# Stick attention masked and summed in one PSUM bank, the delta rule's halves in buffers and a chain of their own, and new words

## The reference

```
z = einsum('bhqd,bhkd->bhqk', qb, k) * scale          # 8 heads of 64
strict = k_pos[None, :] < q_pos[:, None]
log_beta = log_sigmoid(z)
log_keep = where(strict, log_sigmoid(-z), 0.0)
later = cumsum(log_keep, axis=3, reverse=True) - log_keep
w = where(strict, exp(log_beta + later), 0.0)
out = einsum('bhqk,bhkd->bhqd', w, v)
```

## Time and profile before

| | |
|---|---|
| median of 3 runs | 2432.87 us (2431.02 to 2443.61) |
| the profiled execution | 2449.8 us, of which the span from first to last instruction is 2448.0 us |
| TensorE, matmul busy | 2325.2 us (95%), 14918 records |
| VectorE, ScalarE, GpSimd busy | 1556.2 us (64%), 1135.5 us (46%), 430.6 us (18%) |
| chain that ended last | TensorE 87%, VectorE 7%, ScalarE 4%, issue 2% |
| mean granted TensorE clock | 0.966 of full speed |
| mean busy share of the 16 DMA engines | queue 1, 35% of their span |

### The profile page before, as it was taken

How to read it: one execution, slowest core, us unless ns; L and a number is a source line. 1 busy time by engine, 2 the same in 40 slices (tenths; PEclk the granted TensorE clock), 3 DMA queues, 4 the chain that set the end, 5 groups by cost and what they waited for, 6 DMA issues and landing times.

```text
span 2448.0 us, 37895 instructions
## 1 busy us (share of the span) xinstructions
PE 2325.2 (95%) x14918; PEld 2059.4 (84%) x14918; DVE 1556.2 (64%) x2791; ACT 1135.5 (46%) x2015; POOL 430.6 (18%) x393
## 2 busy tenths in 40 slices
PE   6999999899999999999999889999998998999997
PEld 6888879888888889998888777888888886888886
DVE  6866756587687668557765763546765664345765
ACT  5654563365465453436544422336544522244553
POOL 2420012122122100022200320001221030000223
PEclk9999999999999999999999998989998999799998
DMA  6554413154554541125554103014543301102552
GB/s 245 187 177 148 160 36 121 67 191 179 185 190 181 183 158 68 53 87 196 184 185 149 61 19 114 1 69 160 189 173 114 133 27 72 44 23 97 183 181 86
DMA packets 88738, 310.53 MB, mean 127 GB/s; under 512 B 9840, under 2 KB 12144, under 8 KB 88048
## 3 DMA queue, kind: packets, MB, share of 16 engines
q1 hardware_dynamic: 88272, 305.42, 35.1%
q10 hardware_dynamic: 288, 2.69, 0.3%
HBM read 307.02 MB, written 1.05 MB: 126 GB/s over the span
## 4 chain that ended last, share of the span: by engine, by line
PE 87%; DVE 7%; ACT 4%; issue 2%; POOL 1%; DMA 0%; SPq 0%; DVEq 0%; ACTq 0%; POOLq 0%
PE ps L142 85%; DVE scratch L157 3%; PE ps L147 2%; DVE w_lo L157 1%; ACT w_hi L152 1%; ACT scratch L152 1%; DVE scratch L184 1%; ACT L152 1%; ACT scratch L183 1%; DVE scratch L169 1%; POOL scratch L157 0%; ACT h L152 0%; DVE scratch L163 0%; ACT x L152 0%; DMA ring<-in_w 0%
## 5 line engine op out<-in xcount | busy, mean ns | idle before, releaser
L157 DVE TENSOR_TENSOR w_lo<-ring,w_hi 128x1024 fp32r<-128x1024 f32 (+2 forms) x571 | 693.9, 1230 | 431.1 <-ACT w_hi L152 420.7
L142 PE MATMUL ps<-h,w_hi 128*128 128x512 f32 (+1 forms) x2784 | 876.9, 374 | 31.1 <-DVE h L169 19.0
L152 ACT ACTIVATE w_hi<-ring 128x1024 fp32r<-128x1024 f32 (+2 forms) x571 | 582.5, 1033 | 510.0 <-PE ps L142 502.3
L142 PE MATMUL ps<-h,w_lo 128*128 128x256 f32 x2448 | 690.7, 282 | 0.0
L142 PEld LDWEIGHTS ps<-h,w_hi 128*128 128x128 f32 x2784 | 506.7, 191 | 131.5 <-issue 23.5
L142 PEld LDWEIGHTS ps<-h,w_lo 128*128 128x128 f32 x2448 | 466.9, 191 | 0.0
L142 PE MATMUL ps<-f,w_hi 128*128 128x512 f32 (+1 forms) x1444 | 421.9, 358 | 3.3 <-DVE f L157 3.3
L142 PE MATMUL ps<-f,w_lo 128*128 128x256 f32 x1184 | 333.2, 281 | 0.0
L142 PE MATMUL ps<-consts 128*128 128x128 f32 x2374 | 319.1, 286 | 0.0
L142 PEld LDWEIGHTS ps<-consts 128*128 128x128 f32 x2374 | 299.8, 200 | 14.9 <-issue 9.9
L142 PE MATMUL ps<-scratch 64*128 64x128 f32 (+11 forms) x2016 | 284.8, 314 | 24.4 <-DVE scratch L157 10.1
(11 more groups left out here) (130 smaller groups left out, 2273.5 us busy)
## 6 DMA issues: line engine op xcount, KB each, us to landing
ring<-in_w SPq DMA_DIRECT2D x520, 512.0 KB, 3.3
ring<-in_w SPq DMA_DIRECT2D x48, 384.0 KB, 3.4
ring<-in_w SPq DMA_DIRECT2D x16, 396.0 KB, 5.0
stage_consts<-in_ctwo ACTq DMA_DIRECT2D x1, 1344.0 KB, 5.9
stage_consts<-in_cthree ACTq DMA_DIRECT2D x1, 1281.0 KB, 5.5
stage_consts<-in_cone SPq DMA_DIRECT2D x1, 1211.0 KB, 6.0
ring<-in_w SPq DMA_DIRECT2D x9, 128.0 KB, 2.7
x<-in_x SPq DMA_DIRECT2D x4, 256.0 KB, 4.3
```

What stands on the lines that cost most here:

```text
L142: return self.e.matmul(out, lhsT, rhs, start=start, stop=stop, skip_group_check=free)
L152: return self.e.activation(out, x, func, **k)
L157: return self.e.tensor_tensor(out, a, b, op)
```

## The change

- **Stick attention.** `qb` is scaled by 1/8 when it is evicted. z stays in its bank through step 1: TensorE adds the mask (`strict` is now 0 or -1e30, copied to fp32r on ScalarE once) by a product with the identity; ScalarE makes a = Ln(1 + Exp(-Abs(z))); VectorE makes a = max(z, 0) + a in one instruction; TensorE adds its sums over later keys, with the key itself, negated (`lower`, `ones`), onto z in the same bank; ScalarE takes Exp of it. The second bank, the clamp, VectorE's difference and sum and GpSimd's two masks are gone.
- **Delta rule.** A `DeltaBlock` for each half holds its masked products, inverse and what follows from it; some buffers are shared within it (N2, A4, Zt lie on N8; A2, Td on A8), so the copy of the first product of `ri` 0 waits for the second product too. `rm`, `ri`, `ru` of half 1 are a chain of their own, s. Pt, Q moved to the start of scratch; GpSimd clears them at `ri` 0 in place of `rm` 0, and waits for the block's column products first.
- **Words.** All six are new, with 1021 z: m0 80, c0 85, m1 189, c1 77, b0 281, b1 309. In m0, `ck` 1 to 4 come ahead of the stick attention's first head.

```
-SW = 31000
+SW = 31768
-NCON = 3584
+NCON = 2688
 WEAVE = {
...
-    "m0": ("zzzzpzzzzqzyqzzzzzzzzzzqzkzzzzzkzzzqzpzzzzzkqzzbzzzbzkzzalbvtvkasbbaacbzzzaszctaazcctzsszzatyczz"
-           "zzzstccaatszszzztyzzczzszzzazzzcczzzztazsszzzzzzzztzczczzzzozzzzzzzyyzzzyzzzzzzzzzzzzzzztzzzzzs"
-           "zzzzzzzzzzzzzzzzzzyzyooztsoozoozzzzzooozooooozzzozzzozzzozzzzz"),
...
+    "m0": ("zzpzzzyzzqqzkzzqzzzzzkzzpzzbqbkyqzzzzzzzzzzzzzzzyzzlzbykyakvayvbcaasbtcbycsztacaastcsacytszcatsc"
+           "azccattascztctzzzzzzozzzstszzzzzzzzszzzzootstosozzzozozozoooozzzozzzoozoozozzzz"),
...
-        self.strict = K.const("strict", lambda I: np.concatenate(
-            [np.triu(np.ones((128, 128)), 1), np.ones((128, 128)), np.triu(np.ones((128, 128)), 1)], 1), 384, "one")
-        self.lower = K.const("lower", lambda I: np.tril(np.ones((128, 128)), -1), 128, "one")
-        self.ones = K.const("ones", lambda I: np.ones((128, 128)), 128, "one")
+        self.strict = K.const("strict", lambda I: np.where(np.triu(np.ones((128, 128)), 1), 0.0, NEG), 128, "one")
+        self.lower = K.const("lower", lambda I: -np.tril(np.ones((128, 128))), 128, "one")
+        self.ones = K.const("ones", lambda I: -np.ones((128, 128)), 128, "one")
...
         q, k = T.sq(h), T.sk(h)
-        e.mm(b[:, 0:256], k[:, 0:128], q, True, True)
-        e.mm(b[:, 256:384], k[:, 128:256], q[:, 128:256], True, True).then_inc(*e.up("scores", ("stick", h)))
+        e.wait_ge(*K.at("masks", "strict"))
+        e.mm(b[:, 0:256], k[:, 0:128], q, True, False, free=True)
+        e.mm(b[:, 256:384], k[:, 128:256], q[:, 128:256], False, False, free=True)
+        e.mm(b[:, 0:384].rearrange("p (a k) -> p a k", a=3)[:, 0:3:2, :], K.ident_r, bc(K.strict_r, 2), False, False,
+             free=True).then_inc(*e.up("scores", ("stick", h)))
     elif step == 1:
-        b = K.bank(e, ATT, ("stick", h, "c"))
+        b = K.psum(("stick", h, "z"))
         e.wait_ge(*K.at("kept", ("stick", h)))
-        e.mm(b[:, 0:256], T.lower, a[:, 0:256], True, False, free=True)
-        e.mm(b[:, 128:256], T.ones, a[:, 256:384], False, True, free=True)
-        e.mm(b[:, 256:384], T.lower, a[:, 256:384], True, True, free=True).then_inc(*e.up("summed", ("stick", h)))
+        e.mm(b[:, 0:256], T.lower, a[:, 0:256], False, False, free=True)
+        e.mm(b[:, 128:256], T.ones, a[:, 256:384], False, False, free=True)
+        e.mm(b[:, 256:384], T.lower, a[:, 256:384], False, True, free=True).then_inc(*e.up("summed", ("stick", h)))
...
 def act_stick(e, K, T, h, step):
     a, l = (x[:, 0:384] for x in T.sticks[h % 2])
+    z = K.psum(("stick", h, "z"))[:, 0:384]
     if step == 0:
-        e.wait_ge(*K.at("clamped", ("stick", h)))
+        e.wait_ge(*K.at("scores", ("stick", h)))
         if h >= 2:
             e.wait_ge(*K.at("summed", ("stick", h - 2)))
-        e.then(e.act(a, K.psum(("stick", h, "z"))[:, 0:384], ACT.Abs, scale=64 ** -0.5))
+        e.then(e.act(a, z, ACT.Abs))
         e.then(e.act(a, a, ACT.Exp, scale=-1.0))
         e.act(a, a, ACT.Ln, bias=K.onec).then_inc(*e.up("logs", ("stick", h)))
     elif step == 1:
-        e.wait_ge(*K.at("evicted", ("stick", h, "c")))
-        e.act(l, l, ACT.Exp).then_inc(*e.up("exps", ("stick", h)))
+        e.wait_ge(*K.at("summed", ("stick", h)))
+        if h >= 2:
+            e.wait_ge(*K.at("weighted", ("stick", h - 2)))
+        e.act(l, z, ACT.Exp).then_inc(*e.up("evicted", ("stick", h, "z")))
...
 def dve_stick(e, K, T, h, step):
-    a, l = (x[:, 0:384] for x in T.sticks[h % 2])
-    sc = 64 ** -0.5
+    a = T.sticks[h % 2][0][:, 0:384]
     if step == 0:
-        z = K.psum(("stick", h, "z"))[:, 0:384]
-        e.wait_ge(*K.at("scores", ("stick", h)))
-        if h >= 2:
-            e.wait_ge(*K.at("weighted", ("stick", h - 2)))
-        e.ts(l, z, sc, 0.0, MUL, MIN).then_inc(*e.up("clamped", ("stick", h)))
         e.wait_ge(*K.at("logs", ("stick", h)))
-        e.then(e.tt(l, l, a, SUB))
-        e.stt(a, z, -sc, l, MUL, ADD).then_inc(*e.up("evicted", ("stick", h, "z")))
-    elif step == 1:
-        e.wait_ge(*K.at("summed", ("stick", h)))
-        e.tt(l, l, K.psum(("stick", h, "c"))[:, 0:384], ADD).then_inc(*e.up("evicted", ("stick", h, "c")))
-    else:
+        e.stt(a, K.psum(("stick", h, "z"))[:, 0:384], 0.0, a, MAX, ADD).then_inc(*e.up("kept", ("stick", h)))
+    elif step == 2:
...
+class DeltaBlock:
+    def __init__(self, K, at, G):
+        m3 = lambda i: K.area(at + 512 * i, 512, j=4, t=128)
+        self.M = {n: m3(i) for i, n in enumerate(("N8", "A8", "Ao16", "Ao32", "Rb", "Rk", "Ak"))}
+        self.P1 = m3(7)
+        self.N2 = self.A4 = self.Zt = self.M["N8"]
+        self.A2 = self.Td = self.M["A8"]
...
+        self.by_block = [DeltaBlock(K, OVER + 4608 * i, K.rows[:, 256 * i:256 * i + 256]) for i in range(2)]
...
+        inner = lambda tb: ([("rm", (tb, n)) for n in range(5)] + [("ri", (tb, n)) for n in range(7)]
+                            + [("ru", (tb, n)) for n in range(2)])
+        r += inner(0)
         for tb in range(2):
-            r += ([("rm", (tb, n)) for n in range(5)] + [("ri", (tb, n)) for n in range(7)] + [("ru", (tb, n)) for n in range(2)]
-                  + [("rG", tb)] + [("rP", (tb, j)) for j in range(2)] + [("rS", (tb, c)) for c in range(4)]
+            r += ([("rG", tb)] + [("rP", (tb, j)) for j in range(2)] + [("rS", (tb, c)) for c in range(4)]
                   + [("rY", (tb, j)) for j in range(2)])
-        return {"r": r + some("rO", 2),
+        return {"r": r + some("rO", 2), "s": inner(1),
...
-            e.wait_ge(*K.at("summed", key(m)))
+            e.wait_ge(*K.at("summed", key(2 if m == 1 else m)))
...
-            e.wait_ge(*(K.at("summed", (s, "rY", 0, 1)) if tb else K.at("turned", (s, "rtm", 3))))
+            e.wait_ge(*K.at("turned", (s, "rtm", 3)))
...
-    elif what == "rm" and i == (0, 0):
+    elif what == "ri" and i == (0, 0):
         e.wait_ge(*K.at("turned", (s, "rtm", 3)))
+        for n in [(s, "rp", 4), (s, "gp", 2), (s, "gl")] + [((s, "np", n), t) for n in range(3) for t in range(2)]:
+            e.wait_ge(*K.at("summed", n))
```

More of the change, by code:

```diff
@@ L242, in __init__ @@
         self.vf = make("v_first", 512)
-        mr = make("mask_r", 256, F32R)
-        self.ident_r, self.mask_r = mr[:, 0:128], mr[:, 128:256]
+        mr = make("mask_r", 384, F32R)
+        self.ident_r, self.mask_r, self.strict_r = (mr[:, 128 * i:128 * i + 128] for i in range(3))
         self.st = make("stats", 384)
@@ L1549, in pe_stick @@
         v = lambda k: T.vb[:, k, 64 * h:64 * h + 64]
-        e.wait_ge(*K.at("weights", ("stick", h)))
+        e.wait_ge(*K.at("evicted", ("stick", h, "z")))
         for t in range(2):
@@ L1563, in act_mixer0 @@
             act_masks(e, K, "chunk", T.chunk)
+            e.cp(K.strict_r, T.strict).then_inc(*e.up("masks", "strict"))
     elif what in ("lqa", "lka", "lva", "lvb") and i == 1:
@@ L1614, in dve_mixer0 @@
         e.wait_ge(*K.at("evicted", (T.stage, "R")))
-        evict_cols(e, K, (T.stage, what, i), (T.qbT if what == "qb" else T.kbT)[:, 2 * i:2 * i + 2, :], R=K.R)
+        if what == "qb":
+            e.wait_ge(*K.at("summed", (T.stage, what, i)))
+            b = K.psum((T.stage, what, i))[:, :].rearrange("p (k t) -> p k t", k=2)
+            e.stt(T.qbT[:, 2 * i:2 * i + 2, :], b, 64 ** -0.5, bc(K.R, 2), MUL,
+                  MUL).then_inc(*e.up("evicted", (T.stage, what, i)))
+        else:
+            evict_cols(e, K, (T.stage, what, i), T.kbT[:, 2 * i:2 * i + 2, :], R=K.R)
     elif what in ("qa", "ka"):
@@ L1684, in pool_mixer0 @@
         pool_x(e, K, T.stage, i)
-    elif what == "S":
-        h, step = i
-        a, l = (x[:, 0:384] for x in T.sticks[h % 2])
-        if step == 0:
-            e.wait_ge(*K.at("evicted", ("stick", h, "z")))
-            e.tt(a, a, T.strict, MUL).then_inc(*e.up("kept", ("stick", h)))
-        elif step == 1:
-            e.wait_ge(*K.at("exps", ("stick", h)))
-            e.tt(l, l, T.strict, MUL).then_inc(*e.up("weights", ("stick", h)))
 class Mla:
@@ L1899 @@
 OVER = 9744
-GN = 19472
+GN = 20240
 def block_mask(n, kind):
@@ L2057, in __init__, with block_of @@
                        lambda u: [])
+    def block_of(self, what, i):
+        return self.by_block[i if what == "rG" else i[0] if what in ("rm", "ri", "ru", "rP", "rS", "rY") else 0]
     def chains(self):
@@ L2238, in pe_delta @@
 def pe_delta(e, K, T, what, i, xT):
-    s, l, M = T.stage, T.l, T.M
+    s, l, V = T.stage, T.l, T.block_of(what, i)
+    M = V.M
     if what == "rp":
@@ L2312, in pe_delta @@
             e.wait_ge(*K.at("evicted", key(4)))
-            each(e, b, T.A4, T.P1).then_inc(*e.up("summed", key(5)))
+            each(e, b, V.A4, V.P1).then_inc(*e.up("summed", key(5)))
         elif n in (3, 5):
@@ L2326, in pe_delta @@
             e.wait_ge(*K.at("evicted", key((n - 1, "tr"))))
-            each(e, b, T.Td, T.Zt).then_inc(*e.up("summed", key((n, "r7"))))
```

(7 more changed lines are left out.)

99 lines of the change are left out of this document (46 added, 53 removed).

## The result

The changed kernel takes 2414.83 us (median of 5; 2408.71 to 2417.53) against 2431.24 for the kernel before on the same chip: a ratio of 0.9915, interval 0.9893 to 0.9937, so 16 us less by the medians and 21 by the ratio. A second set of runs gives 0.9929 (0.9911 to 0.9948), 17 us less. The forecast was 2387 and its range ended at 2413. The sign was right, the size was not: the time lies in the range of rival B.

The account below looks back on a forecast made before the run. TensorE, with fill on its path, was taken as the bound; m0 -4, c0 -1, m1 -8, c1 -3, b0 -17, b1 -15, clock +2 gave -46: 2387 us against the median 2432.87. Forecast 2376 to 2402, whole range 2362 to 2413.

Parts of the forecast that it names:

- rival B: Engines behind TensorE (VectorE in the blocks, ScalarE in m0, m1) take back half or more: 2403 to 2421 us, chance 0.18.
- what the fill's time is worth: All stages: 249 fewer fill products issued, at 0.225 us each, give 56 us at most.
- These stay: b0 and b1: the short stretches at 1.2 GHz, as behind `nc`'s products, stay; 2 us added for m0's new waits only.
- The count of fill: Issued z fall by 79 (m0), 6 (c0), 42 (m1), 15 (c1), 53 (b0), 54 (b1): 249 in all.
- m0, forecast -4: m0, stick attention: 79 fill products fewer, 1.8 us of mask products and 12 us of new waits added: -4 us.
- ScalarE late next: m0's packed heads: ScalarE has 36 us of work against TensorE's 33; followed head by head, 12 us of new waits.
- b0, forecast -17: b0, delta rule halves: 12 us from less fill and 5 us from bare waits gained: -17 us.
- The gap between 1417 and 1467: b0: second-half pieces fill TensorE's waits there; of 10 us of bare waits 5 are gained, VectorE late next.
- b1, forecast -15: b1, delta rule halves: 10.5 us from less fill and 4.5 us from bare waits gained: -15 us.
- b1 over 365 us: Sign that the prediction is wrong: b0 or b1 takes over 365 us.
- m1, c0, c1, forecast -12: m1, c0, c1: order and fill alone, nothing computed differently: -8, -1 and -3 us.
- D's mechanism: From `nc` to the output product of b0, b1: less fill puts more small products at 1.2 GHz; slower, chance 0.05.

Follow-up runs that it names:

- e_trim_m1: e_ck_between with less fill in m1, c0 and c1 (71 of 189 z in m1, 7 and 4 in c0 and c1): 2402.1 us, ratio 0.9846 to the kernel before.
- p_stick: The kernel before with only the new stick attention and the new word of m0: ratio 1.0033 to the kernel before, 8 us more.
- e_no_ln: The changed kernel without the eight Ln of the stick attention, so the weights are not the reference's: 2390.7 us, ratio 0.9814 to the kernel before.
- e_ck_between: The changed kernel with two of the four `ck` weight products moved back among the heads of m0: 2401.5 us, ratio 0.986 to the kernel before.
- p_m1c: The kernel before with only the new words of c0, m1 and c1: ratio 0.9949 to the kernel before, 12 us less.
- e_old_b: The changed kernel with the old words of b0 and b1 on the new buffers: ratio 0.9976 to the kernel before.
- p_blocks: The kernel before with only the delta rule's new buffers and chain and the new words of b0 and b1: ratio 0.9913, 21 us less.

## Why the prediction was wrong in size

- **The step that failed: what the fill's time is worth.** The prediction took fill that ends behind its release for time on the path, and gave back little for it: 2 us for the clock ("These stay") and, all stages together, 4 for bare waits. Over the six stages the fill came out as forecast, -56 us for -54. But real work rose by 15 us where the sum has 4, with the clock in m0 and b1, and bare waits by 12 where it has 4. That leaves 28 of the 46 us in the profiles. e_trim_m1 tests the reading directly: 16 us of such fill gave 0. It isn't wrong everywhere: in m1, c0 and c1 the change took out 11 us of fill and they got 10 shorter.
- **The count of fill: the total is right, by luck.** The prediction put all but one of the 67 z that aren't issued behind the last TensorE piece of b0 and b1. The trace shows those 32 and 34 issued, and the 39 and 43 of the new words too. The ends of b0, before and after (two records for each product):

```profile
1654.67 7.31 PE L142 MATMUL ps<-consts 128*128 128x128 f32 x64
1630.02 9.27 PE L140 MATMUL ps<-consts 128*128 128x128 f32 x78
```

  The z that find no free bank stand elsewhere, and their numbers happen to be the same, 67 and 83. Counted by word in the records, m1 has 26 fewer where 42 were forecast, b0 71 where 53 were.
- **m0, forecast -4, measured +1.6 in the profiles; p_stick's ratio says +8 for the part.** The order of late engines was right: ScalarE late next, TensorE waiting on it. The waits were over-sized (12 us forecast, 5 measured net), and the longest, of 3.2 us, is a wait for z's bank, which the prediction didn't follow. The clock was left out: +2 for it in the sum, 15 measured (e_no_ln). The mask product was small, as forecast; e_ck_between shows m0 can be 11 us shorter than before with it.
- **b0, forecast -17, measured -15.** A right total from two wrong terms: fill -17.5 in place of -12 (the wrong count), and bare waits +4.8 in place of -5. The gap between 1417 and 1467 didn't close: over the same distance from the stage's start TensorE is busy 40.7 of 50 us, as it was 40.2. Of b0's bare waits 18 to 20 us ended on VectorE before, 22 to 27 after. VectorE's work is the same 200 us, now in less time.

```profile
1413.00:1463.00 50.00, 40.70 (x272) 32.56 (x270) 27.05 (x68) 14.83 (x23) 5.87 (x6) 0.90 0.11 35
```

- **b1, forecast -15, measured -5.** Fill -12.4 (10.5 forecast); bare waits +1.6 in place of -4.5; and real work +5.6, where the sentence "these stay" stood for the clock. The stretch behind the compression grew from at most 24 us to 27 to 44 in eight of nine profiles, from a cause that is open. The prediction had named b1 over 365 us as a sign of being wrong, and it came: 368.
- **m1, c0, c1, forecast -12, measured -10 in the profiles and -12 by p_m1c.** The number is right; the count under it was not (49 fewer products counted by word, 63 forecast).
- **The base.** Against the median the sum was too large by what before's profiled execution lost in the blocks by a lower clock (0.92 against 0.95 in p_stick and e_old_b). A sum made against it couldn't be carried over to the median in full.
- **The rivals.** B's number came true, for half of its reason: VectorE took back in the blocks, but in m0 it was the clock more than ScalarE's waits. D's mechanism was at work: 35 us more at 1.2 GHz in all (166 to 201 us in the two profiles). The argument against it took one stretch, looked for gaps inside it and not ahead of it, and took it for all.

## What to carry to other kernels

Before you take fill out, ask what the engine's clock does without it, and try the removal on one stage: here 16 us of fill behind its releases gave nothing, and 25 products put into three waits gave 9 us. When an order is packed, look for the engine with the longest work for a unit of it (ScalarE, with its table loads) and keep dense work of the bound engine between the units: moving two weights back was worth 13 us of m0. In m0 a gap cost twice, once as a wait and once as the clock behind it. And when a result is left in its bank for a later step, ask what needs that bank next in the ring.

## What the runs showed of the hardware

- In m0 of the changed kernel TensorE stood bare for 4.3 of 21 us, at 2.4 GHz; the last gap was one of 3.2 us, and from within it on came 31 us at 1.2 GHz, in which it was busy 28. The same products without gaps ran at 2.4 GHz among the heads (e_no_ln).
- The same instructions in the same order ran b1 in 354, in 368 and in 380 us (p_blocks, the changed kernel, e_trim_m1), b0 of the old word in 363 and in 372, with the granted clock lower in the longer ones: one profiled execution is a sample.
- A stretch at 1.2 GHz can begin with no wait ahead of it: b1 of the changed kernel, 44 us at 0.50 with TensorE busy 44.
- A table load takes 1.28 us, and each of the eight heads paid for two (17 loads in m0, one in e_no_ln). The Trainium skill (ScalarE: Activation LUTs, What ACT_TABLE_LOAD costs) has 2.66 us with its drain; in m0 the next operation starts 1.29 us after the load does (338.10 to 339.39), so the measured figure stands.
